# Two-block transformer step on one core: layer-norm parts behind the seams, key blocks ahead of the transposes, and the selected attention two blocks later

## The reference

```python
for l in range(DEPTH):                                    # DEPTH = 2
    x = layer_norm(DN_ALPHA * x + 0.5 * swiglu_ffn(x, ffn_w_in[l, 0], ffn_w_out[l, 0]), ln_g[l, 0], ln_b[l, 0])
    x = layer_norm(DN_ALPHA * x + mixer_sublayer(x, ...), ln_g[l, 1], ln_b[l, 1])
    x = layer_norm(DN_ALPHA * x + memory_cross_attention(x, mem, ...), ln_g[l, 2], ln_b[l, 2])
    x = layer_norm(DN_ALPHA * x + 0.5 * swiglu_ffn(x, ffn_w_in[l, 1], ffn_w_out[l, 1]), ln_g[l, 3], ln_b[l, 3])

def mixer_sublayer(x, w_in, b_gate, ..., w_branch, w_out, rel_bias):
    (qa, ckv, iq, ik, iw, qs, ks, vs, cb, cc, ch, ga, gb, gc) = jnp.split(x @ w_in, offsets, axis=-1)
    y_a = dsa_branch(qa, ckv, iq, ik, iw, w_uk, w_uv, rel_bias)     # selected attention
    y_b = stick_breaking_branch(qs, ks, vs)
    y_c = short_conv_branch(cb, cc, ch, conv_w)
    merged = (jax.nn.sigmoid(ga + b_gate[0]) * (y_a @ w_branch[0]) + jax.nn.sigmoid(gb + b_gate[1]) * (y_b @ w_branch[1])
              + jax.nn.sigmoid(gc + b_gate[2]) * (y_c @ w_branch[2]))
    return merged @ w_out
```

## Time and profile before

| | before |
|---|---|
| median of 3 runs | 2734.07 us (2733.89 to 2734.32) |
| the profiled execution | 2733.68 us, span 2731.9 us |
| PE busy | 2581.6 us, 94% |
| DVE busy | 1699.6 us, 62% |
| ACT busy | 1256.9 us, 46% |
| mean granted PE clock | 0.976 of full |

### The profile page before, as it was taken

One profiled execution on the slowest core, in us unless ns is written; L12 is line 12 of the kernel. 1 busy time (PEld: TensorE's weight loads), 2 busy tenths in 40 slices (PEclk: granted clock), 3 DMA queues, 4 the chain that ended last, 5 costly groups with the idle time before them and its releaser, 6 DMA issues. The chain is left out here.

```text
span 2731.9 us, 48808 instructions
## 1 busy us (share of the span) xinstructions
PE 2581.6 (94%) x16525; PEld 2222.4 (81%) x16525; DVE 1699.6 (62%) x2507; ACT 1256.9 (46%) x1798; POOL 173.9 (6%) x215
## 2 busy tenths in 40 slices
PE   8999989999999999899999998899999998879899
PEld 8998877889888878787788876687898896656898
DVE  4556766765465465767775767776666566645555
ACT  4435445444344345454554553455444443533443
POOL 1000000010010000000010201200000011100000
PEclk9999999999999999999999999999999999989999
DMA  7655546467576564455566434553556757325664
GB/s 234 210 176 161 145 150 187 165 206 260 185 222 216 182 214 124 149 157 193 171 205 181 151 113 151 174 155 104 166 178 194 232 180 213 124 93 183 198 187 135
DMA packets 276178, 479.68 MB, mean 176 GB/s; under 512 B 17616, under 2 KB 87320, under 8 KB 275872
## 3 DMA queue, kind: packets, MB, share of 16 engines
q1 hardware_dynamic: 265632, 445.24, 51.4%
q0 software_dynamic: 10304, 31.31, 3.8%
HBM read 475.33 MB, written 6.92 MB: 177 GB/s over the span
## 5 line engine op out<-in xcount | busy, mean ns | idle before, releaser
L122 DVE TENSOR_TENSOR wlo<-raw,whi 128x1024 fp32r<-128x1024 f32 (+3 forms) x786 | 911.8, 1172 | 737.1 <-ACT whi L163 600.3
L163 ACT ACTIVATE whi<-raw 128x1024 fp32r<-128x1024 f32 (+3 forms) x786 | 786.2, 1015 | 599.1 <-PE bank L171 431.9
L171 PE MATMUL bank<-xh,whi 128*128 128x256 f32 x2208 | 633.5, 287 | 11.0 <-DVE xl L122 10.8
L171 PE MATMUL bank<-xl,whi 128*128 128x256 f32 x2208 | 625.3, 283 | 0.0
L171 PE MATMUL bank<-xh,wlo 128*128 128x256 f32 x2208 | 625.2, 283 | 0.0
L171 PEld LDWEIGHTS bank<-xh,whi 128*128 128x128 f32 x2208 | 422.9, 192 | 27.1 <-issue 19.7
L171 PEld LDWEIGHTS bank<-xl,whi 128*128 128x128 f32 x2208 | 422.7, 191 | 1.1 <-issue 0.5
L171 PEld LDWEIGHTS bank<-xh,wlo 128*128 128x128 f32 x2208 | 422.3, 191 | 0.0
L171 PE MATMUL bank<-whi,xh 128*128 128x512 f32 (+2 forms) x632 | 255.6, 404 | 19.1 <-issue 10.4
L171 PE MATMUL bank<-whi,xl 128*128 128x512 f32 (+2 forms) x632 | 249.0, 394 | 0.0
L171 PE MATMUL bank<-wlo,xh 128*128 128x512 f32 (+2 forms) x632 | 248.6, 393 | 0.0
(11 more groups left out here) (432 smaller groups left out, 3905.1 us busy)
## 6 DMA issues: line engine op xcount, KB each, us to landing
raw<-in_ffn_w_in SPq DMA_DIRECT2D x280, 512.0 KB, 4.5
raw<-in_ffn_w_out SPq DMA_DIRECT2D x154, 512.0 KB, 4.5
raw<-in_w_mix_in SPq DMA_DIRECT2D x112, 512.0 KB, 3.6
raw<-in_mod_w SPq DMA_DIRECT2D x96, 512.0 KB, 5.4
raw<-in_od_w_in SPq DMA_DIRECT2D x40, 512.0 KB, 4.7
raw<-in_ffn_w_in SPq DMA_DIRECT2D x56, 256.0 KB, 2.9
raw<-in_w_branch SPq DMA_DIRECT2D x24, 512.0 KB, 3.6
raw<-in_ev_w_in SPq DMA_DIRECT2D x24, 512.0 KB, 4.2
```

The lines of the kernel that those rows point to most:

```text
L122: return Made(self.e and self.e.tensor_tensor(out, a, b, op))
L163: return Made(self.e and self.e.activation(out, a, f, **k))
L171: return Made(self.e and self.e.matmul(out, lhs, rhs, **k))
```

## The change

1. In `LayerNorm.steps` the scales of tile 1's second and third part are written in a row, and the rounding and `xl` of these parts behind them; in a keep seam a weight block is staged ahead of the second part's rounding, and the next one behind the last `xl`.
2. `between_layers` writes tile 0's transposes ahead of the filler only if `keep`. In the two mixer-to-cross seams the keys' two blocks now stand first, and then both tiles' transposes.
3. `choose` yields after the rounds 1, 3 and 5 instead of 2 and 5; `dsa` gives two more turns away after `"room"`.
4. The second half of `w_mix_out` is done by `gemm` and no longer by `gemm_by_tile`.

```diff
@@ LayerNorm.steps
-        half = [self.low(first[0][0], 0, 0, 4, first[0][1])]
-        for k0, nk, b, m in second:
+        def scaled(k0, nk, b, m):
             co.dv.wait_ge(m, co.lncdep)
             for k in range(nk):
                 o, (g, s) = b.ap[:, k * P:(k + 1) * P], self.column(k0 + k)
                 v = co.dv.tensor_scalar(o, o, g, s, ALU.mult, ALU.add).then_inc(co.s_dv)
-            a = self.high(b, 1, k0, nk, v)
-            if k0 == 0:
-                half.append(self.low(first[1][0], 0, 4, 4, first[1][1]))
-            elif co.keep:
-                stage_part(co)
-            co.xt.dep += [(half[k0 // 4], self.low(b, 1, k0, nk, a))] * (nk // 2)
+            return v
+
+        def parts(i, v):
+            k0, nk, b, m = second[i]
+            return self.low(b, 1, k0, nk, self.high(b, 1, k0, nk, v))
+
+        half = [self.low(first[0][0], 0, 0, 4, first[0][1])]
+        v = scaled(*second[0])
+        half.append(self.low(first[1][0], 0, 4, 4, first[1][1]))
+        co.xt.dep.append((half[0], parts(0, v)))
+        v, last = scaled(*second[1]), scaled(*second[2])
+        if co.keep:
+            stage_part(co)
+        co.xt.dep.append((half[0], parts(1, v)))
+        co.xt.dep += [(half[1], parts(2, last))] * 2
+        if co.keep:
+            stage_part(co)
@@ between_layers
     steps = norm.steps()
-    next(steps)
+    if keep:
+        next(steps)
     co.keep = keep
@@ choose
-            if r in (2, 5):
+            if r in (1, 3, 5):
                 yield
@@ dsa
         while "room" not in dep:
             yield
+        yield
+        yield
@@ the end of mixer
-    run(co, gemm_by_tile(co, xt, mdep, A["w_mix_out"][l], 512, res(0, 512), 0, 8))
+    run(co, gemm(co, xt, mdep, A["w_mix_out"][l], 512, 512, res(0, 512)))
```

## The result

The changed kernel takes 2709.15 us (median of 4 runs, 2705.23 to 2713.73), the kernel before 2733.98 in the same session; the ratio is 0.9911, with a 95% interval of 0.9893 to 0.9929. The direction was right, the size was missed by a factor of three. The profiled execution took 2707.20, 26.5 less than that of before.

What follows compares the result with a forecast made beforehand. PE, busy 94% of the span, bounds the kernel: its work, idle and half-clock losses. 3.9 - 0.3 + 5.1 = 8.7 us off 2733.68 gives 2725.0; adjusted to the median, 2725.5, range 2715 to 2732.5.

Steps and rivals of the forecast that it cites:

- part 3: Selected attention, two layers: idle 14.7 to 12.0 gives 2.7 us, fewer half-clock stretches 2.4, together 5.1.
- Part 1: Five keep seams: last waits for `xl` fall at 778, 985 and 1349, 3.9 us gained in sum.
- The walk of 985: Keep seam at 985: with the scales moved ahead, the later block starts at 995.7, not 997.64, gaining 1.9 us.
- The two early seams: Keep seams at 205 and 570: half clock for 6.8 us behind the transposes, PE waits for nothing, gain 0.
- Rival D: Keep seams: the change does nothing to a seam since staging in `stage_part` wasn't late; the prediction excluded it.
- Parts 2 and 4: Two mixer-to-cross seams: 6.1 us of old losses go, new `xk` waits come; 0.6 in layer 0, -0.9 in layer 1, sum -0.3.
- Rival A: Mixer-to-cross seams: bank waits don't bind, so 6.1 us twice instead of -0.3, giving 2713 us; chance 0.10.
- the transposes' wait: Selected attention: transposes of `dsl` wait for bank 0, read by the second gates' `sg`; 2.7 us.
- save most of the other, 1.2: Selected attention: one of two half-clock stretches behind the first wait mostly goes, 1.2 of its 1.7 us per layer.
- Rival B: Attentions and mixer-to-cross seams: each new wait leaves two half-clock stretches, so 2735.9 us, slower; chance 0.16.
- Rival C: Only the keep seams move; attention waits stay 14.7 us and mixer-to-cross seams give zero: 2729.8 us; chance 0.12.
- My own sign of being wrong: Rest of the kernel, whose order is the same: the forecast is wrong if it moves by more than 4 us.

Runs made afterwards that it cites:

- the first profile: Profiled execution of the changed kernel, all parts in: 2707.20 us, with a measured median of 2709.15 us.
- the second profile: The changed kernel profiled once more, unedited: 2710.27 us, ratio 0.9918 to the kernel before.
- the banks made free: Changed kernel with the keys' two banks marked as last used when read out, so q takes other banks: 2702.90 us, ratio 0.9888 to the kernel before.
- part 3 alone: Kernel before with only the selected-attention edits (picks in four steps, dsa two turns later): 2718.65 us, ratio 0.9950.

## Why the prediction was wrong

- **Direction and places: right.** All waits that it named appeared in the first profile, with their releasers. The sizes were wrong, most of all in part 3.
- **Part 1, 3.9 forecast:** 5.2 in the first profile, 7.1 in the second, 6.6 measured alone. The walk of 985 (1.9) was right where the clock was full: 2.2 alone and 2.1 in the second profile, but 0.2 in the first, where it fell to half. (Two of its sums are off by little: 992.6 and 2.95 are 995.55, not 995.7, and the two `xl` end at 993.3, not 993.0.) The two early seams, which I had at 0 since half clock covered them, gave 0.6 and 1.6 to 1.9. At 570 the half clock lasted 6.8 us before and 3.4 after. Rival D, that the seam wouldn't move, fell.
- **Parts 2 and 4, -0.3 forecast:** +0.4 and +0.3. The step from the list of banks to the wait for `xk`, and the sign of each layer, held. The wait in layer 0 was 1.0 shorter than I had it: DVE was through with `xk` 0.6 sooner than by the sum of its rows, and PE came 0.4 later, since it waited 0.42 at the transposes. Rival A (banks don't bind) fell; with the banks made free the seams are worth 5.8 per layer.
- **Part 3, 5.1 forecast:** 15.1, less 1.2 behind it; 13.7 measured alone. This is the term that failed, in two of its numbers.
  - First, "**2.7**" for the transposes' wait: measured 0.97 and 0.72 in the first profile, 0 and 0.75 in the second. The prediction names the smaller pick steps, but its 2.7 is what the kernel without them has (2.9 and 2.7 with the turns alone); the finer picks take about 2 us out of that wait (3.3 to 1.3 alone, 2.9 to 0.97 beside the turns). In layer 0 the walk gave DVE 17.0 us from the end of the first gates' adds to the end of the second (356.3 to 373.3) and PE 14.3 up to the transposes; the trace has 16.1 and 15.1, and these two together are the 1.7. With the small change that didn't come, idle fell from 14.7 to 7.7 in both layers and not to 12.0.
  - Second, "save most of the other, 1.2": the six stretches of half clock in both layers became two, so the clock gave 3.4 a layer and not 1.2. I had one stretch behind the first wait, which came, and one behind the second, which didn't. How much of that is the change's isn't settled: the second profile of the changed kernel has three such stretches, and part 3 alone the four that I had forecast. Why a stretch follows one wait and not another stays open; the runs show the number, not the reason.
- **Rival B (the clock takes the gain) fell** the other way: there were fewer stretches, not more. **Rival C (only the keep seams move) fell** with part 3.
- **The profile that I started from** had the short wait for `lb` in layer 1 (2.8, against 4.3 to 4.6 in four of six executions). What part 3 takes away there is therefore larger than any sum from that profile could show, by up to 2.7 us.
- **The rest,** about 7 us in the first profile and 5 in the second, in parts of the kernel whose order is the same, I had at 0. My own sign of being wrong (more than 4 us there) thus came. It isn't shown to be the change's: in two profiles of the kernel before, the stretch from 1560 to 1900 moved by +2.8 and that from 1900 to 2330 by -1.1. The three parts measured alone add up to the whole, but only within some 6 us, which settles nothing on this term. What remains open is whether a kernel with fewer waits early also meets fewer stretches later by more than chance.
- **The range** was too narrow at its low end for the same reason: the upper end of part 3 (9) assumed that the second wait brings no stretch, but kept its length of 2.7.

## What to carry to other kernels

When two edits touch one queue, walk the queue with both in; the 2.7 that I gave the second wait was that of a kernel with one of the two edits. Where PE is the bound, an idle stretch avoided can be worth more than its length: in layer 0 here 3.4 us of idle took 3.4 us of half clock along, in other executions of the same order less. This term deserves a range of its own, and a second profile of the kernel before shows how wide. Where banks are handed out by age, an edit far ahead changes who collides: list the bank and its last reader at each product behind the edit, and don't expect that moving a bank repairs a wait: it did for the keys and didn't for the gates, where the wait came back at another bank.

## What the runs showed of the hardware

The scatter of one program was larger than the first three runs had it: they lay within 0.43 us, while 23 later runs of the kernel before lay between 2724.22 and 2737.01. Two executions of the same program had half clock at different seams behind equal waits. In the kernel with the turns alone, a wait of 2.87 us in layer 0 was followed by full clock and one of 2.70 at the same place of layer 1 by a clock of 0.50; behind one of 2.79 in the changed kernel it fell to 0.53. So a wait's length alone didn't decide it. And the same DMA of the bias, in the same program, landed within 5.2 us in one execution and within 6.7 in another.
